# A two-layer network on one Trainium2 core: the MLP down-projection by 7 block products in 18 passes, its right operands split on chip, and the activation differences made on GpSimd

## Chip, core and metric

The kernel runs on 1 core of one Trainium2 chip. The metric is device time in microseconds (us) of one launch; the time before is the median of 3 runs. Engines are named as in the profile: PE is TensorE (matmuls), PEld its weight load, DVE VectorE, ACT ScalarE, POOL GpSimd, and SP the engine that issues most DMAs. A name with q behind it is that engine's queue.

## What is computed

The input is one sequence of 1024 tokens with width 1024, float32. Two residual layers and a mixed-attention block follow one another:

```python
for i in range(2):
    mod = silu(c) @ ada_w[i] + ada_b[i]
    sh1, sc1, g1, sh2, sc2, g2 = split(mod, 6)
    h = modulate(rmsnorm(x, norm_mix_g[i]), sh1, sc1)
    x = x + g1 * mixer_i(h)                # pooling in layer 0, a gated spatial unit (SGU) in layer 1
    h = modulate(rmsnorm(x, norm_mlp_g[i]), sh2, sc2)
    x = x + g2 * (square(relu(h @ mlp_w1[i])) @ mlp_w2[i])
x = rmsnorm(x, final_g)
x = x + attention_block(x)                 # two kinds of attention, 16 heads
out = rmsnorm(x, final_norm_gain)
```

The MLP is 1024 to 4096 to 1024. Every large product is made in three matmuls: both operands are split into a rounded high part (type fp32r) and the rest, and hi*hi, hi*lo and lo*hi are added up in PSUM.

## The kernel before

All activations lie transposed in SBUF: width on the partitions in 8 row tiles of 128, tokens along the free side in two halves of 512. One program per engine is written by a common walk over the steps (`walk`, from the middle of the file), and the order on each engine is the order of the calls in it. Semaphores carry all waits. The stage buffer `stage` has 4 slots of 1 MB and takes weights in the order of the walk.

**Up stage** (`fast`, 14 phases a layer). h @ w1 is made per 256 hidden columns as a 2x2 block product by 7 products instead of 8 (`PRODUCTS`, L47, the Winograd form of Strassen's method). The right sides are quarters of h and four sums T1 to T4 of them, made once a layer. The left sides are four quarters of the weight unit and sums S1 to S4, made on DVE (L1953) in every phase. ACT rounds each left side (L1389), DVE makes its low part (L1932). DVE joins the products in PSUM and SBUF (L1970), ACT applies relu and the square (L1408, L1410) and rounds (L1413), DVE makes the low part (L1976), and SP stores both parts to `hidden` in HBM (L871), 512 KB per tile. The first two units of a layer (`first_up`, `first_tile`) are made in the plain way. A phase is 84 matmuls.

**Down stage** (`down`, 16 chunks a layer). Chunk c takes 256 rows of w2 and the two hidden tiles of each half (`MB`, already in high and low parts) and makes 16 output tiles, each with 6 matmuls (L2341 to L2343), in 4 PSUM banks. DVE adds each to the residual, X = X + gate * product (L2035): 256 a layer. ACT and DVE split the weight unit once a chunk (L1223, L1696). 1536 matmuls a layer. In layer 0 SP also brings the modulation weights of layer 1 in chunks 1 to 14 (`late`): 16 units of 1 MB, each of which DVE takes in two instructions of 1024 columns (L1674, L1677), and `mods` on PE (L2362) sums them over the partitions. In the last chunk the squares, sums and statistics of the next norm are made between the output tiles (`completed`).

**Around it.** `norm` scales each of the 16 tiles on DVE (L1853), ACT rounds it (L1259), DVE makes the low part (L1861). Behind the MLP of layer 0 come the value columns of the SGU (`values`, L2656 to L2658, 384 matmuls: 8 token tiles, two units of weights for each of two column halves, statistics on DVE at L2047), then `spatial`, four rounds of `gates` and `mix`, and `project`. Behind the MLP of layer 1 come the heads of the attention block.

The wait that matters on PE in `fast` is this one: the fifth and sixth of the PE products wait for what DVE has joined.

```python
if q == 4:
    pe.wait_ge(first_copied, g + 1)
if q == 5:
    pe.wait_ge(joined, 5 * g + 2)
if q == 6:
    pe.wait_ge(joined, 5 * g + 3)
```

Of the kernel before, what the change touches and what calls it, by code (L numbers as in the profile page):

```python
# [18 lines left out]
P = 128  # L19
S = 1024  # L20
# [25 lines left out]
SUMS = ("T1", "T3", "T2", "T4")  # L46
PRODUCTS = (("S1", "T1", "D", True), ("A11", "B11", "A", True), ("S2", "T2", "B", True), ("S3", "T3", "C", True),  # L47
            ("A12", "B21", "A", False), ("A22", "T4", "C", False), ("S4", "B22", "D", False))
BLOCKS = (("22", 1, 1), ("11", 0, 0), ("21", 1, 0), ("12", 0, 1))
# [22 lines left out]
for _name, _n in (("ident", P), ("tri", P), ("pairs", P), ("rot", P), ("invc", 4 * 16)):  # L72
# [8 lines left out]
         "combine first_up first_tile fetch ops fast fetched_ada fetched_split finish").split()  # L81


class Tally:
# [3 lines left out]
    def __init__(self):  # L88
        self.n = dict.fromkeys("u w c uc un a d t h b q s st n sp ada mod x g o ol r v v2 vg f".split(), 0)
        self.reg, self.per = None, {}  # L90
        self.lead = 0
        self.stored = [0] * SLOTS
# [24 lines left out]
    def loop(self, eng, count, per, body):  # L117
# [6 lines left out]
        for name in self.n:  # L124
            assert name == "uc" or self.n[name] == start[name] + per.get(name, 0), name
            self.n[name] = start[name] + count * per.get(name, 0)

# [8 lines left out]
def build(nc, x_in, cols_in, const_in, ada_w, pool_w, sgu_in, sgu_ws, sgu_bs, sgu_out, w1, w2,  # L136
# [4 lines left out]
    def sb(name, shape, dt=F32, at=None):  # L141
# [3 lines left out]
        if at is None:  # L145
# [25 lines left out]
    MB = sb("MB", [P, 2, FT, NH, 2 * H], F32R)  # L171
# [16 lines left out]
    m_slot = {"22": sb("slot22", [P, 2, H], F32R, at=x_at + 12 * S), "11": sb("slot11", [P, 2, H], F32R, at=x_at + 20 * S),  # L188
              "21": sb("slot21", [P, 2, H], F32R, at=x_at + 28 * S), "12": sb("slot12", [P, 2, H], F32R, at=acc_at + 4 * S)}
    m_full = {"22": sb("full22", [P, H], at=x_at + 16 * S), "11": sb("full11", [P, H], at=x_at + 24 * S),  # L190
              "21": sb("full21", [P, H], at=acc_at), "12": sb("full12", [P, H], at=acc_at + 2 * S)}
    U1 = sb("U1", [P, H], at=x_at + 18 * S)
    U2 = sb("U2", [P, H], at=x_at + 26 * S)
    first_full = sb("first_full", [P, 2, H], at=acc_at)
    first_slot = sb("first_slot", [P, 2, H], F32R, at=acc_at + 4 * S)
    S_sum = sb("S_sum", [P, H], at=acc_at + 8 * S)
    later_full = sb("later_full", [P, 2, H], at=x_at)
    later_slot = sb("later_slot", [P, 2, H], F32R, at=x_at + 4 * S)
# [23 lines left out]
    w_at = m_at + 32 * S  # L222
    rows = sb("rows", [1, 2, D], at=w_at + 4 * UNIT)
# [45 lines left out]
    hidden = nc.dram_tensor("hidden", (F // P, NH, P, 2 * H), F32).ap()  # L269
# [33 lines left out]
    def down_tile(c, i):  # L303

        first = 3
        if c > 0:
            return i // KT, i % KT
        if i < 2 * first:
            return i // first, i % first
        return (i - 2 * first) // (KT - first), first + (i - 2 * first) % (KT - first)  # L310

# [4 lines left out]
    def first_places(i):  # L316

        full, slot = (first_full, first_slot) if i < 4 else (later_full, later_slot)
        return full[:, i % 2, :], slot
# [14 lines left out]
    def hidden_tiles(c, hf):  # L334

        return MB[:, c % 2, :, hf, :].bitcast(F32), hidden[2 * c:2 * c + 2, hf].rearrange("f p n -> p f n")

# [24 lines left out]
    def ada_total(l, cc):  # L362

        return X[:, 2, :] if (l, cc) in ((0, 5), (1, 0), (1, 1)) else acc[:]

    def stats(hf, order="down"):

        return PS_ALL[:, 5, :] if order == "pooled" and hf == 1 else (B6, A[:, 1, :])[hf]

    def pair_of(hf, v):  # L370

        return stats(hf)[:, 0:8].rearrange("p (t v) -> p v t", v=2)[:, v, :]
# [4 lines left out]

    def sums(order, hf):
        return SUM if order == "down" or hf == 0 else SUM2
# [53 lines left out]
    x_loaded = [sem(f"x_loaded{k}") for k in range(KT)]  # L433
# [36 lines left out]
    qk_loaded = [sem(f"qk_loaded{i}") for i in range(2)]  # L470
    v_loaded = [sem(f"v_loaded{i}") for i in range(2)]
    bias_loaded = [sem(f"bias_loaded{i}") for i in range(2)]
# [2529 lines left out]
```

## Time and profile before

| what | us |
|---|---|
| median of 3 runs (lowest, highest) | 2523.53 (2520.54, 2524.2) |
| span of the profiled execution | 2519.7 |
| PE busy | 2460.9 (98%) |
| DVE busy | 1636.2 (65%) |
| ACT busy | 986.4 (39%) |
| POOL busy | 273.9 (11%) |
| the chain that ended last, on PE | 87% |

The span runs from the first to the last instruction of one execution; for that execution no other time is listed, so the span is set beside the runs. Matmuls overlap one another, so a PE duration of 0.39 us is a latency, and what a matmul costs is the distance from its start to the next one's. The same holds in part for DVE and ACT.

### The profile page before, as it was taken

What the parts mean: (1) busy time and instruction counts of PE and PEld (TensorE: products, weight loads), DVE (VectorE), ACT (ScalarE), POOL (GpSimd) and SP (SyncE); (2) the same over time, 40 slices, a digit from 0 to 9 for tenths busy, and PEclk for the clock granted to TensorE, in tenths of its full rate; (3) what the DMA queues carried; (4) which work ended last, traced back from release to release, by engine and by line L of the source; (5) the groups of instructions that cost most, each with busy time, mean ns of one, the idle gap of its engine ahead of it and who ended that gap; (6) DMA issues with size and microseconds to landing.
All of it is one profiled execution on the core that took longest, in us unless ns stands there. A gap on an engine that the chain in (4) does not pass through costs nothing.

```text
span 2519.7 us, 32563 instructions
## 1 busy us (share of the span) xinstructions
PE 2460.9 (98%) x11616; PEld 2003.8 (80%) x11616; DVE 1636.2 (65%) x2554; ACT 986.4 (39%) x1622; POOL 273.9 (11%) x279
## 2 busy tenths in 40 slices
PE   7999999999999999999999999999999999999998
PEld 2588888788887888888888888888888897886677
DVE  7798776777776343458667666666651226998873
ACT  2366565000003232237666300001431226887851
POOL 0200000000002000100000000000010002557731
PEclk9899999999999999999999999999999999999999
DMA  8726666855543610333544844431334472346621
GB/s 306 267 76 234 226 223 260 317 190 178 200 167 108 178 46 1 134 117 142 192 159 167 317 176 140 145 134 51 126 121 146 143 184 71 85 111 160 168 68 67
DMA packets 219076, 396.89 MB, mean 158 GB/s; under 512 B 59440, under 2 KB 136368, under 8 KB 218928
## 3 DMA queue, kind: packets, MB, share of 16 engines
q1 hardware_dynamic: 203696, 336.21, 40.3%
q10 hardware_dynamic: 15232, 58.72, 6.4%
q8 instruction: 91, 1.49, 0.2%
q14 instruction: 57, 0.47, 0.1%
HBM read 285.83 MB, written 115.08 MB: 159 GB/s over the span
## 4 chain that ended last, share of the span: by engine, by line
PE 87%; DVE 5%; issue 3%; POOL 3%; ACT 1%; DMA 0%; DVEq 0%; POOLq 0%; ACTq 0%; SPq 0%
PE banks L2341 23%; PE banks L2343 23%; PE banks L2342 23%; PE banks L2432 2%; PE banks L2871 2%; PE banks L2889 2%; PE banks L2656 1%; PE banks L2657 1%; PE banks L2658 1%; POOL probs L1139 1%; PE banks L2495 1%; DVE neg_max L2278 1%; PE banks L2373 1%; PE banks L2858 1%; PE banks L2859 1%
## 5 line engine op out<-in xcount | busy, mean ns | idle before, releaser
L2035 DVE SCALAR_TENSOR_TENSOR X<-banks,mod,X 128x512 f32<-128x512 f32 x512 | 380.8, 749 | 227.2 <-PE banks L2343 227.0
L2341 PE MATMUL banks<-Hhi,Whi 128*128 128x512 f32 x1248 | 493.3, 395 | 6.6 <-DVE Hlo L1861 2.9
L2342 PE MATMUL banks<-Hlo,Whi 128*128 128x512 f32 x1248 | 486.8, 390 | 0.0
L2343 PE MATMUL banks<-Hhi,Wlo 128*128 128x512 f32 x1248 | 486.8, 390 | 0.0
L2341 PE MATMUL banks<-MB,Whi 128*128 128x512 f32 x1024 | 401.5, 392 | 2.2 <-DVE X L2035 2.2
L2343 PE MATMUL banks<-MB,Wlo 128*128 128x512 f32 x1024 | 399.5, 390 | 0.0
L2342 PE MATMUL banks<-MB,Whi 128*128 128x512 f32 x1024 | 399.4, 390 | 0.0
L1223 ACT ACTIVATE Whi<-stage 128x2048 fp32r<-128x2048 f32 x59 | 112.9, 1913 | 615.3 <-PE banks L2343 577.2
L2341 PEld LDWEIGHTS banks<-Hhi,Whi 128*128 128x128 f32 x1248 | 235.1, 188 | 59.6 <-issue 8.3
L2342 PEld LDWEIGHTS banks<-Hlo,Whi 128*128 128x128 f32 x1248 | 235.1, 188 | 50.4 <-issue 2.4
L2343 PEld LDWEIGHTS banks<-Hhi,Wlo 128*128 128x128 f32 x1248 | 234.9, 188 | 49.4
L2341 PEld LDWEIGHTS banks<-MB,Whi 128*128 128x128 f32 x1024 | 192.9, 188 | 42.5 <-issue 3.0
L2343 PEld LDWEIGHTS banks<-MB,Wlo 128*128 128x128 f32 x1024 | 192.8, 188 | 40.4
L2342 PEld LDWEIGHTS banks<-MB,Whi 128*128 128x128 f32 x1024 | 192.9, 188 | 39.2
L1696 DVE TENSOR_TENSOR Wlo<-stage,Whi 128x1024 fp32r<-128x1024 f32 (+1 forms) x93 | 145.2, 1562 | 89.6 <-ACT Whi L1223 88.1
L1139 POOL TENSOR_SCALAR probs<-probs,rden 128x1024 f32<-128x1024 f32 (+2 forms) x128 | 118.3, 924 | 337.3 <-DVE rden L2284 327.6
L2289 DVE TENSOR_TENSOR PTl<-banks,PTh 128x512 fp32r<-128x512 f32 (+2 forms) x256 | 135.2, 566 | 6.6 <-ACT PTh L1609 5.5
L2871 PEld LDWEIGHTS banks<-const,probs 128*128 128x128 f32 x800 | 88.6, 140 | 56.8 <-DVE PTl L2289 22.6
L2341 PE MATMUL banks<-T,Whi 128*128 128x512 f32 x336 | 131.1, 390 | 0.0
L2871 PE MATMUL banks<-const,probs 128*128 128x128 f32 x800 | 116.5, 279 | 14.7 <-POOL probs L1139 9.2
L1609 ACT ACTIVATE PTh<-banks 128x512 fp32r<-128x512 f32 (+2 forms) x256 | 119.5, 504 | 29.1 <-PE banks L2871 26.2
L2343 PE MATMUL banks<-T,Wlo 128*128 128x512 f32 x336 | 130.8, 389 | 0.0
(247 smaller groups left out, 3773.2 us busy)
## 6 DMA issues: line engine op xcount, KB each, us to landing
stage<-w SPq DMA_DIRECT2D x64, 1024.0 KB, 6.1
hidden<-slot SPq DMA_DIRECT2D x112, 512.0 KB, 3.0
MB<-hidden ACTq DMA_DIRECT2D x56, 1024.0 KB, 5.6
stage<-ada_w SPq DMA_DIRECT2D x48, 1024.0 KB, 6.5
x_saved<-X SPq DMA_DIRECT2D x32, 512.0 KB, 3.1
stage<-w_in SPq DMA_DIRECT2D x13, 1024.0 KB, 6.2
X<-x_saved SPq DMA_DIRECT2D x24, 512.0 KB, 7.2
MB<-hidden SPq DMA_DIRECT2D x8, 1024.0 KB, 10.1
```

Source lines behind the costliest of these rows:

```text
L1139: nc.gpsimd.tensor_scalar(out=row, in0=row, scalar1=rden[:, u % 4:u % 4 + 1], scalar2=1.0, op0=ALU.mult, op1=ALU.mult).then_inc(probs_scal ...
L1223: nc.scalar.activation(Whi[:, T.n["w"] % 2, :], stage[:, s, :], ACT.Copy).then_inc(w_hi, 1)
L1609: nc.scalar.activation(probs_t(PTh, u, kind, first, m), TP[:, g, 0:m * P] .rearrange("p (k q) -> p k q", q=P), ACT.Copy).then_inc(th_done, 1)
L1696: ins = nc.vector.tensor_tensor(Wlo[:, w % 2, at], stage[:, u % STAGES, at], Whi[:, w % 2, at].bitcast(F32), ALU.subtract)
L2035: nc.vector.scalar_tensor_tensor(out=X[:, k, half(hf)], in0=Dn[:, i % D_BANKS, :], scalar=gate[:, k:k + 1], in1=X[:, k, half(hf)], op0=ALU ...
L2289: nc.vector.tensor_tensor(probs_t(PTl, u, kind, first, m), TP[:, g, 0:m * P].rearrange("p (k q) -> p k q", q=P), probs_t(PTh, u, kind, fir ...
L2341: nc.tensor.matmul(out_bank, whi, xhi, start=start, stop=False, skip_group_check=onto)
L2342: nc.tensor.matmul(out_bank, whi, xlo, start=False, stop=False, skip_group_check=onto)
L2343: return nc.tensor.matmul(out_bank, wlo, xhi, start=False, stop=stop, skip_group_check=onto)
L2432: ins = nc.tensor.matmul(row_bank(cc, h), c_act[:, 2 * q + k:2 * q + k + 1], stage[:, u % STAGES, k * D + h * H:k * D + (h + 1) * H], star ...
L2871: ins = nc.tensor.transpose(TP[:, g, k * P:(k + 1) * P], PE_[:, u % 2, a:a + P], con("ident"))
L2889: ins = nc.tensor.matmul(OB[:, g % 2, :], VT[:, e, k, :], x[:, g % 2, k, :], start=k == tiles[0] and x is PTh, stop=k == tiles[-1] and x i ...
```

## The change

The down-projection becomes a 2x2 block product too. An output block pair `o` (4 of them) is 256 rows of the width by 1024 tokens; a pair `p` (16 of them) is 256 rows of w2. A pass makes the 7 products of one `o` over 2 to 4 `p`, and adds them to X and to a running sum UT. 18 passes of 42, 63 or 84 matmuls make 1344 a layer. The right sides are now stored unsplit, 7 tiles of 256 KB a pair (B11, B21, B22 and T1 to T4), brought back one by one (`load_raw`, a ring of 8) and split on chip: ACT rounds, DVE makes the low part. The four differences T1 to T4 of the up stage's results are made on POOL (on DVE for the first two units), and so are the weight sums S1 to S4 of each pass. Modulation vectors 2, 3 and 4 of layer 1 move to the value stage of the SGU, and vector 5 into the up stage of layer 1. The norm behind the down stage begins after the last pass.

```diff
+PASSES = ((0, 0, 2), (1, 0, 3), (2, 0, 4), (3, 0, 4), (0, 2, 6), (1, 3, 7), (2, 4, 8), (3, 4, 8), (0, 6, 10),
+          (1, 7, 11), (2, 8, 12), (3, 8, 12), (0, 10, 14), (1, 11, 14), (2, 12, 16), (0, 14, 16), (1, 14, 16),
+          (3, 12, 16))
...
+def made_during(p):
+    return -1 if p < 2 else p - 2 if p < 4 else max(t for t in range(NPASS) if PASSES[t][1] <= p - 4 < PASSES[t][2])
+def right_steps(t):
+    pairs = [p for p in range(CHUNKS) if made_during(p) == t]
+    steps = [[] for _ in range(len(SIDES) + 1)]
+    for n, p in enumerate(pairs):
+        for q in range(len(SIDES)):
+            steps[min(q + 2 * n, len(SIDES))].append((p, q))
+    return steps
...
+            for t in range(NPASS):
+                do["passes"](T, gate, l, t, base, then)
...
         do["values"](T, 0, range(1))
+        for q in range(4):
+            ada(1, 2, q)
         split(src_values(1, 0))
         do["values"](T, 0, range(1, 8))
+        for q in range(4):
+            ada(1, 3, q)
         split(src_values(1, 1))
         do["values"](T, 1, range(5))
+        for q in range(4):
+            ada(1, 4, q)
         split(src_in(sgu_in, 0))
...
+            if j < 3:
+                mods(1, 2 + j)
...
+            def load_raw(T, l, n):
...
+                    sync.wait_ge(right_lo, split_by(l, p0, q0))
+                side_stored(l, p, q)
+                sync.dma_start(raw_tile(T, n), hidden[p, q]).then_inc(raw_in[n % RAW], 16)
...
@@ SP @@
+            def passes(T, gate, l, t, base, then):
+                if t + 2 < NPASS:
+                    load_pass(T, l, t + 2)
+                if t == 0:
+                    sync.wait_ge(m_square, 4 * g + 1)
+                    sync.wait_ge(joined, 5 * g + 3)
+                    reload_row(3)
+                    for n in range(4):
+                        store_sum(PAIRS - 1, g, n)
...
+                    for k, b, name in ((4, "22", "T2"), (5, "11", "T1"), (7, "21", "T4")):
+                        sync.wait_ge(b_stored[b], 16 * (g + 1))
+                        sync.wait_ge(t_stored[name], 16 * (g + 1))
+                        reload_row(k)
+                for n in LOADS[t]:
+                    load_raw(T, l, n)
...
@@ POOL @@
+            def fast(T, l, p, base, unit, last):
+                for n in range(4 if p > 0 else 0):
+                    hidden_sum(T.n["f"] - 1, n)
+                if last:
+                    pass_sums(T, l, 0, ("S1", "S3", "S2", "S4"))
@@ POOL @@
+            def passes(T, gate, l, t, base, then):
+                if t + 1 < NPASS:
+                    pass_sums(T, l, t + 1, ("S1", "S3", "S2"))
+                    for n in range(4 if t == 0 else 0):
+                        hidden_sum(g, n)
+                    pass_sums(T, l, t + 1, ("S4",))
...
@@ ACT @@
+            def passes(T, gate, l, t, base, then):
...
+                for q in range(len(SIDES)):
+                    act.wait_ge(pass_done, 7 * (NPASS * l + t) + q + 1)
+                    if q == 1 and t == FIRST_PASS[o]:
+                        nc.scalar.activation(UT[:, o, :], fast_bank("A", t), ACT.Copy).then_inc(u_begun, 1)
+                    if t + 1 < NPASS:
+                        pass_hi(T, l, t + 1, base, q)
+                    for p, r in steps[q]:
+                        right_hi(T, l, p, r)
...
@@ DVE @@
+            def passes(T, gate, l, t, base, then):
...
+                for q, name in enumerate(("D1", "A1", "B", "C1", "A2", "C2", "D2")):
+                    if name in evictions(t):
+                        evict(l, t, gate, name)
+                    if q == 2 and last:
+                        for more in ("U21", "U12", "U22"):
+                            evict(l, t, gate, more)
+                    if t + 1 < NPASS:
+                        pass_lo(T, l, t + 1, base, q)
+                    for p, r in steps[q]:
+                        right_lower(T, l, p, r)
...
@@ PE @@
+            def passes(T, gate, l, t, base, then):
+                if t == 0:
+                    pe.wait_ge(joined, 5 * T.n["f"])
...
+                for q, (_, side, bank, first) in enumerate(PRODUCTS):
+                    pe.wait_ge(ps_lo, 7 * n + q + 1)
...
+                    if q == 4:
+                        if t == FIRST_PASS[o]:
+                            pe.wait_ge(u_begun, OUTS * l + t + 1)
...
+                    if q == 5:
+                        pe.wait_ge(evicted, evicted_by(l, t, "C1"))
```

## Rows read from the trace of the kernel before

**Rows 1.** The page: busy time by engine, and the granted clock in 40 slices.
```profile
PE 2460.9 (98%) x11616; PEld 2003.8 (80%) x11616; DVE 1636.2 (65%) x2554; ACT 986.4 (39%) x1622; POOL 273.9 (11%) x279
PEclk9899999999999999999999999999999999999999
```

**Rows 2.** Stretches: us, busy us by engine (instructions), granted clock, DMA share, GB/s.
```profile
437.86:803.87 366.01, 362.29 (x1625) 300.26 (x1623) 263.13 (x330) 42.08 (x36) 15.57 (x11) 0.99 0.54 192
803.87:810.64 6.77, 3.83 (x25) 3.59 (x25) 6.77 (x12) 4.92 (x9) 1.53 (x2) 0.86 0.97 335
1419.20:1780.16 360.96, 360.96 (x1649) 300.89 (x1648) 228.61 (x298) 43.07 (x38) 0.00 (x0) 1.00 0.42 153
```

**Rows 3.** Groups on PE; then two PE starts, 35 matmuls apart.
```profile
L2341 PE MATMUL banks<-MB,Whi 128*128 128x512 f32 x1024 | 401.5, 392 | 2.2 <-DVE X L2035 2.2
437.86 0.39 PE L2341 MATMUL banks<-MB,Whi 128*128 128x512 f32 x1
445.79 0.39 PE L2343 MATMUL banks<-MB,Wlo 128*128 128x512 f32 x1
```

**Rows 4.** Groups on DVE: instructions, busy us, mean ns, idle before.
```profile
L2035 DVE SCALAR_TENSOR_TENSOR X<-banks,mod,X 128x512 f32<-128x512 f32 x512 | 380.8, 749 | 227.2 <-PE banks L2343 227.0
L1976 DVE TENSOR_TENSOR slot<-full,slot 128x512 fp32r<-128x512 f32 x112 | 77.0, 687 | 41.6 <-ACT slot L1413 41.6
L2289 DVE TENSOR_TENSOR PTl<-banks,PTh 128x256 fp32r<-128x256 f32 x96 | 37.6, 418 | 4.5 <-ACT PTh L1609 3.5
L1677 DVE SCALAR_TENSOR_TENSOR acc<-stage,c_act,acc 128x1024 f32<-128x1024 f32 x24 | 31.7, 1322 | 0.9
```

**Rows 5.** Groups on ACT, and the subtractions' nearest kin on POOL.
```profile
L1389 ACT ACTIVATE Whi<-stage 128x512 fp32r<-128x512 f32 x112 | 69.6, 621 | 41.0 <-PE banks L2343 40.8
L1077 POOL TENSOR_TENSOR SUM<-SUM,SQ x38: 1266/1288/2252, 91.1 to 2503.6; 128x512 f32<-128x512 f32 x38
L1132 POOL TENSOR_TENSOR ws<-ws,const 128x128 f32<-128x128 f32 x8 | 3.4, 461 | 37.2 <-DMA bs<-sgu_bs 37.2
```

**Rows 6.** Timeline: DVE instructions that start beside one on POOL.
```profile
1844.66 1.28 DVE L2227 TENSOR_TENSOR RF<-COS,RT 128x512 f32<-128x512 f32 x1
1844.10 1.29 POOL L1125 TENSOR_TENSOR COS<-QN,rope 128x512 f32<-128x512 f32 x1 [6.84 <-DVE QN L2217]
783.42 2.17 DVE L1696 TENSOR_TENSOR Wlo<-stage,Whi 128x1024 fp32r<-128x1024 f32 x1
780.89 8.69 POOL L1077 TENSOR_TENSOR SUM<-SUM,SQ 128x512 f32<-128x512 f32 x5 [0.80 <-ACT SQ L1239]
```

**Rows 7.** DVE timeline in one up phase with a modulation unit.
```profile
361.93 1.28 DVE L1674 SCALAR_TENSOR_TENSOR X<-stage,c_act,X 128x1024 f32<-128x1024 f32 x1
371.00 0.69 DVE L1970 TENSOR_TENSOR U<-banks,U 128x512 f32<-128x512 f32 x1 [0.40 <-PE banks L2343]
380.96 1.28 DVE L1674 SCALAR_TENSOR_TENSOR X<-stage,c_act,X 128x1024 f32<-128x1024 f32 x1
```

**Rows 8.** DMA issues: number, KB each, us from issue to landing.
```profile
q_heads<-OL SPq DMA_DIRECT2D x16, 256.0 KB, 2.3
X<-x_saved SPq DMA_DIRECT2D x16, 256.0 KB, 3.5
stage<-ada_w SPq DMA_DIRECT2D x48, 1024.0 KB, 6.5
```

**Rows 9.** DVE timeline in the value stage: statistics and weight splits.
```profile
855.85 0.69 DVE L2047 BATCH_NORM_STATS2 bstat<-V 128x6 f32<-128x512 f32 x1 [2.03 <-ACT V L1452]
857.66 2.29 DVE L1696 TENSOR_TENSOR Wlo<-stage,Whi 128x2048 fp32r<-128x2048 f32 x1 [1.11 <-ACT Whi L1223]
891.21 0.69 DVE L2047 BATCH_NORM_STATS2 bstat<-V 128x6 f32<-128x512 f32 x1 [12.91 <-ACT V L1452]
```

**Rows 10.** PE timeline: end of the values, start of the gates; a restart after idling.
```profile
898.55 1.88 PE L2620 MATMUL banks<-ws,ones 128*128 128x512 f32 x4
899.87 0.80 PE L2341 MATMUL banks<-Hhi,Whi 128*128 128x512 f32 x1
116.12 0.77 PE L2341 MATMUL banks<-Hhi,Whi 128*128 128x512 f32 x1 [2.91 <-DVE Hlo L1861]
119.24 0.42 PE L2342 MATMUL banks<-Hlo,Whi 128*128 128x512 f32 x1
```

More of the change, by code:

```diff
@@ L597, in walk, with mlp @@
         T.n["un"] = T.n["u"]
-        def mlp(l, with_ada, after, then):
+        def mlp(l, after, then):
             base = T.n["c"] % 2
@@ L1075, in add_squares @@
                     reach(pool, stat_done, T("st", 2 * hf if order == "down" else 0))
-                first = SQ[:, (i - 1) % 2, :] if k == 1 else acc_sum[:]
-                nc.gpsimd.tensor_tensor(acc_sum[:], first, SQ[:, i % 2, :], ALU.add).then_inc(sum_done, 1)
+                if order == "blocks" and hf == 1 and k == 1:
+                    pool.wait_ge(evicted, evicted_by(T.n["e"] // NPASS, LAST_PASS[OUT_ORDER[1]], "U22"))
+                before = sq_tile(order, i - 1) if k == 1 else acc_sum
+                nc.gpsimd.tensor_tensor(acc_sum, before, sq_tile(order, i), ALU.add).then_inc(sum_done, 1)
             def constant_term():
@@ new lines, in passes @@
+            def passes(T, gate, l, t, base, then):
+                g = PAIRS * (l + 1) - 1
+                if t + 1 < NPASS:
[3 more added lines that the diff above has]
+                    pass_sums(T, l, t + 1, ("S4",))
+                if then == 2:
+                    for n, o in enumerate(OUT_ORDER):
+                        if t == min(LAST_PASS[o] + 1, NPASS - 1):
+                            for i in range(4 * n, 4 * n + 4):
+                                add_squares(T, "blocks", i)
@@ L1204, in attend_end @@
                 gated(T, -1, KT - 1)
-            walk(pool, dict(start=start, pool=pool_step, down=down,
+            walk(pool, dict(start=start, pool=pool_step, fast=fast, passes=passes,
                             spatial=spatial, project=project, heads=heads, attend=attend,
@@ L1349, in project, with block_square @@
+            def block_square(T, l, i, then):
+                act.wait_ge(evicted, finished(l, i))
+                square(T, "blocks", i, then == 4)
             def project(T, j, gate, first, then=None):
@@ L1638, in attend_end @@
                 lower_half(T, -1)
-            walk(act, dict(start=start, prepare=prepare, v_a=v_a, split=split, fetched_split=split, opening=opening,
-                           norm=norm, pool=pool, down=down, values=values, gates=gates,
+            walk(act, dict(start=start, prepare=prepare, v_a=v_a, split=split, opening=opening,
+                           norm=norm, pool=pool, passes=passes, values=values, gates=gates,
                            combine=combine, first_tile=first_tile, ops=ops, fast=fast,
@@ L1882, in norm @@
                                             ALU.subtract).then_inc(gap_ready, 1)
-                    invert(T, 0)
-                for n in range(begun, 2 * KT + 2):
-                    if n == (6 if order == "pooled" else begun + 2):
+                invert(T, 0, which == 4)
+                for n in range(2 * KT + 2):
+                    if n == (6 if order == "pooled" else 2):
                         invert(T, 1, which == 4)
@@ L2469, in norm @@
                 if which == 4:
-                    both_stats(T, 14)
-                    both_stats(T, 15)
+                    for i in range(12, 2 * KT):
+                        both_stats(T, i)
                 elif order == "pooled":
                     pooled_seven(T, 1)
-                    pe.wait_ge(tb_ready, T("b"))
-                    spread(T, 0, B7)
+                elif order == "blocks":
+                    for hf in range(NH):
+                        first_seven(T, order, hf)
+                        eighth(T, order, hf)
                 else:
```

664 lines of the change are left out of this document (410 added, 254 removed).

## The prediction

> **What bounds the kernel.** I read the busy times first: PE is busy for 98% of the span at a granted clock near full speed, the next engine, DVE, for 65% [rows 1]. The stretches then say that this holds in the stage that changes: in layer 1 the down stage lasts 360.96 us with PE busy throughout, and DVE is busy for 228.61 of them [rows 2]. So matmuls taken out there are time, as long as DVE, ACT, POOL and the loads keep up. PE's list shows what one costs: 35 starts in 7.93 us, 0.227 us each, not the 0.39 us of its duration [rows 3]. The other engines' groups give the prices of the work put in [rows 4, 5].
>
> **What is removed.** 1536 - 1344 = 192 matmuls a layer, 384 x 0.227 = 87.2 us off PE. On DVE 256 additions to X a layer become 134 (seven a pass, less four that ACT makes, and three more where each of the four outputs ends), but each pass adds 7 low parts of weights, and eleven passes add 7 (three of them 14) low parts of right sides.
>
> **The up stage.** DVE loses four low parts a phase, ACT four roundings; POOL gains four differences. A POOL instruction of 512 columns is 1.29 us [rows 5]. DVE and POOL do not run freely side by side: a DVE subtraction of two SBUF tiles that began 0.56 us after a POOL product took 1.28 us where its kind takes 0.69, and ended 0.55 us after POOL did; one of 1024 columns took 2.17 us beside five POOL additions, which themselves took 8.69 us [rows 4, 6]. So the four differences, early in the next phase, can hold DVE for up to 4 x 1.15 = 4.6 us. Phases follow at 380.96 - 361.93 = 19.03 us [rows 7]. The join of the fourth product started at 371.00, 0.40 us after DVE was free, and the product that waits for it was due some 2.4 us later; two low parts ahead of it (1.2 us) are gone. 0.4 + 1.2 + 1.8 = 3.4 us of slack against 4.6: a slip of up to 1.2 us in each of the 16 phases that have a modulation unit (12 in layer 0, 4 now in layer 1); the other phases have 2.6 us more slack and slip by nothing. I take 0.5 us, as part of the 4.6 falls where DVE waits anyway: **+8** (0 to 20).
>
> The Trainium skill (SBUF — State Buffer, Who interferes with whom) states that the pair of ports is locked for a whole instruction, and that the later of a two-input DVE instruction and a GpSimd reader fully blocks. By that rule the slip is the full 1.2 us, +19 in place of +8; the pair at 1844 agrees with it, to 0.13 us.
>
> **The start of the down stage.** In the last phase POOL makes its four differences (from about 2.9 us into the phase, 4 x 1.33) before S1 of the first pass, so ACT's first rounding comes at 9 us where it was free at 3, and all operands behind it are late: about 3 us at the sixth product. PE also waits for the last join (0.2 + 0.69 us). **+4** a layer (1 to 8).
>
> **Pass 0.** Here I expect the largest loss. SP's program of this pass puts the four stores of the last differences, and waits for three of them to have landed, ahead of the first raw tile of pair 2. ACT has that tile in its order at step 0, ahead of the copy that starts UT, and PE's fifth product waits for the copy. From the start of the pass: S2 of the next pass is made at 3.9 us (product 1.4, rounding 0.6, low part 0.6, POOL 1.1), four differences to 9.2, the last store landed at 11.7 (2.3 for 256 KB [rows 8]), three row loads and the raw load issued by 12.4, landed at 15.9 (3.5 [rows 8]), ACT's two instructions to 17.1. The fifth product was due at 5.4: 11.7 us of idling, and some 2.5 more at the sixth, since DVE then has four right sides and three left sides to make up. **+14** a layer; 0 if these waits are met early, 20 if the raw tile queues behind three 512 KB rows.
>
> **Passes 1 to 17.** A pass of n pairs is 21n matmuls: 9.5, 14.3 or 19.1 us. DVE's instructions in a row cost 0.66 us (addition), 0.61 (512 columns) or 0.35 (256; durations 749, 687, 418 ns [rows 4], less 0.07 of overlap). Pass with n = 4 and 7 right sides: 4.6 + 4.3 + 4.3 = 13.2, or 18.5 with all of POOL's four sums (5.3) against it: covered. With 14 right sides (passes 3, 7, 11): 17.4 to 22.7 against 19.1. Pass 1: 12.6 to 17.9 against 14.3; pass 13 13.2 to 18.5 against 14.3. Pass 16 is short and ends an output: 10.9 to 16.2 against 9.5. Summed, the least is 1.4 and the most 25 us a layer; I take **+8** in layer 0, where POOL's norm additions lie in the last passes, and **+6** in layer 1. ACT stays under DVE throughout (0.62 us each [rows 5]).
>
> **Ends of the down stages.** Before, layer 0 ran 437.86 to 803.87 and then 6.77 us to the next matmuls [rows 2], 372.8 together, with four modulation sums of PE (7.4) and statistics in it. After: 305.1 (1344 x 0.227) + 4 + 14 + 8 + 7 for the last addition, square, statistics, root, spread and first tile, + 1.3 for DVE's scaling of the second half = 339.4; the sums move, 7.4, and three of them now wait 0.8 us for ACT's evictions: 349.2. **-23.6**. Layer 1: 360.96 + 2.6 of statistics = 363.6; after 305.1 + 4 + 14 + 6 + 9.7 (12 statistics) + 6.6 = 345.4: **-18.2**, of which 4 us are given back because the norm begins only after the last pass.
>
> **Value stage.** DVE gets 12 units of 2 x 1.26 us there. PE asks for the fourth weight unit at 866.6, 48 x 0.227 = 10.9 us after its half begins at 855.7; before, its low part was done at 857.66 + 2.29 [rows 9]. Now four units (10.1) stand ahead of it, and its load starts only when the first of them frees its slot (856.5 + 2.5), lands 6.5 us later [rows 8], and ACT 1.9 and DVE 2.3 follow: 869.9 where 866.6 was due, **+3.3**. The gates' unit has to follow the statistics of 891.21 [rows 9] and four units: 891.9 + 10.1 + 2.3 = 904.3, where the gates began at 899.87 [rows 10]: **+4.5**. Together +8 (0 to 14); nothing on PE covered it.
>
> **Clock.** After 2.91 us of idling PE's matmuls came 0.43 us apart for eight of them, twice the normal distance: the 1.2 GHz level in place of 2.4 [rows 10]. Such a restart costs 1.6 us; I count three: **+5**.
>
> **Sum.** 2519.7 - 23.6 - 18.2 + 8 + 8 + 5 = 2498.9 of span; the median of the runs stands 3.8 above the profiled span: **2503 us**, 0.8% less.
>
> **Rivals.**
> - The forecast: a fifth of the 87 us stays, the rest goes into fixed places, pass 0 first. Chance 0.47.
> - The first pass does not stall, because the differences are early or the stores land fast, and PE restarts less: 2503 - 28 - 5 = 2470. For it: stores of this size land in 2.3 us at a DMA share of 0.42 [rows 2, 8]. Against it: POOL's order and SP's put everything in one line. Chance 0.21.
> - A wash: everything given back, pass 0 at 18 us and the other passes at 12 a layer: 2503 + 8 + 10 = 2521. For it: the queues behind 512 KB rows. Against it: two terms have to be high together. Chance 0.13, of which 0.11 within 0.2%.
> - Slower by the port: each POOL difference holds DVE where it has no slack. The point is the join of the fourth product: if it starts later than 13 us into a phase, PE slips one for one. One POOL instruction of 1.29 us lost in each of 26 phases (33.5, 8 counted) and 0.65 in 26 passes (17): 2503 + 42 = 2545. For it: 2.17 us in place of 1.22. Against it: unaided phases have 6 us of slack. Chance 0.19. The row at 783.42 shows 0.95 us of such holding [rows 6]. By the lock rule of the Trainium skill (SBUF — State Buffer, Who interferes with whom) every POOL instruction that reads SBUF holds such a DVE instruction in full, which leads to this case.
>
> Faster means by over 0.2% (5 us, about what a measurement of this kernel can tell). Faster 0.68, same 0.11, slower 0.21. The range 2470 to 2540 leaves out the far ends of the second and last case.
>
> **What would show it.** After: 2688 matmuls in the passes, and PE waiting for UT's copy (ACT) in the first pass, over 10 us a layer; ACT waiting there for a DMA from hidden; the join rows of 1.2 us and more in the up stage; PE waiting for DVE's weight split twice in the value stage; gaps of some 5 us in passes 1, 15 and 16. The forecast is wrong if the first pass of a layer lasts under 12 us, or if PE idles by over 1 us a phase in the up stage.

## The result, and the profile after

The changed kernel takes 2567.57 us (median, 2562.71 to 2570.25), the kernel before, run beside it, 2522.86 us. The ratio is 1.0175 with a 95% interval of 1.016 to 1.0189: slower by 1.75%, where 2503 us, faster, was predicted, with 2540 as the upper end. The profiled execution has a span of 2564.1 us, 44.4 more than before.

The page of the changed kernel, its busy times and the granted clock, answers to [rows 1]:

```profile
PE 2419.3 (94%) x11232; PEld 1958.2 (76%) x11232; DVE 1708.7 (67%) x2610; ACT 1111.1 (43%) x1946; POOL 661.2 (26%) x535
PEclk9899999899998988999999989999999999999999
```

384 matmuls are gone, as the change says. But PE is busy for 94% of a longer span, and the clock row shows eights where it had nines. At 0.227 us each they are worth 87.2 us; so the change costs 131.6 us elsewhere. The stretches of the changed kernel say where (us, busy us by engine, granted clock, DMA share, GB/s). In order: up stage of layer 0, its down stage up to the value columns, the values, gates to project, up and down stage of layer 1:

```profile
116.47:453.79 337.32, 325.28 (x1440) 265.95 (x1440) 278.13 (x337) 167.22 (x287) 90.70 (x56) 0.99 0.50 171
453.79:802.59 348.80, 317.76 (x1393) 260.75 (x1393) 250.76 (x365) 139.59 (x250) 121.41 (x84) 0.96 0.46 153
802.59:912.08 109.49, 94.86 (x391) 76.40 (x390) 66.97 (x80) 31.74 (x38) 5.36 (x8) 0.92 0.64 202
912.08:1144.93 232.85, 227.32 (x1058) 193.16 (x1057) 85.12 (x117) 54.68 (x78) 15.49 (x12) 0.91 0.25 81
1144.93:1468.36 323.43, 314.99 (x1386) 258.87 (x1385) 243.74 (x318) 170.09 (x286) 86.56 (x56) 1.00 0.46 161
1468.36:1824.33 355.97, 328.85 (x1481) 272.26 (x1481) 249.59 (x371) 139.97 (x252) 103.23 (x72) 0.96 0.46 153
```

The same stretches before, with the change that the terms of the prediction gave each and the change that came:

| stretch | before | predicted | measured |
|---|---|---|---|
| up stage, layer 0 | 321.7 | +10 | +15.6 |
| down stage and transition, layer 0 | 372.8 | -37.4 | -24.0 |
| values | 89.2 | +8 | +20.3 |
| gates to project | 206.8 | +7.9 | +26.0 |
| up stage, layer 1 | 312.5 | +7.9 | +10.9 |
| down stage and transition, layer 1 | 363.6 | -22.2 | -7.6 |
| clock, not placed | | +5 | in the above |
| the rest, with the opening | 853.0 | 0 | +3.2 |
| sum | 2519.7 | -20.8 | +44.4 |

Every stretch is worse than its term, and the largest miss, 18 us, is in a stage whose matrices the change doesn't touch. PE's waits (what it waited for: us in total, times, longest):

```profile
PE banks L2651 <- ACT UT L1602: 37.4, 2, 18.9
PE banks L2651 <- DVE U L2241: 17.4, 18, 3.1
PE banks L2651 <- DVE X L2325: 11.2, 8, 3.7
PE banks L2941 <- POOL ws L1379: 8.8, 1, 8.8
PE banks L2977 <- DVE Wlo L1972: 5.9, 1, 5.9
PE banks L2674 <- ACT X L1739: 2.3, 3, 0.8
```

They name four suspects: the copy to UT in pass 0 (foreseen), the joins of the up stage (foreseen, smaller), the spatial weights (not foreseen), and three short waits of 0.8 us in the gates, which look like nothing.

### The profile page after: what moved, and what is told of

It is laid out like the page before. It is cut to its first block, busy times and chain, and to the rows that moved or that the text cites. A ratio compares the mean times of both kernels' runs of the same rounds, so it can differ in the third digit from the quotient of the medians.

```text
span 2564.1 us, 32727 instructions
## 1 busy us (share of the span) xinstructions
PE 2419.3 (94%) x11232; PEld 1958.2 (76%) x11232; DVE 1708.7 (67%) x2610; ACT 1111.1 (43%) x1946; POOL 661.2 (26%) x535
## 4 chain that ended last, share of the span: by engine, by line
PE 71%; DVE 12%; issue 10%; POOL 4%; ACT 2%; DMA 1%; POOLq 0%; DVEq 0%; SPq 0%; ACTq 0%
PE banks L2651 19%; PE banks L2653 19%; PE banks L2652 19%; DVE Wlo L2203 2%; PE banks L3192 2%; PE banks L3210 2%; PE banks L2729 2%; POOL probs L1386 1%; DVE S_sum L2224 1%; PE banks L2793 1%; PE banks L3179 1%; PE banks L3180 1%; DVE U L2241 1%; DVE stage L2224 1%; PE banks L2685 1%
## 5 line engine op out<-in xcount | busy, mean ns | idle before, releaser
L2651 PE MATMUL banks<-Hhi,Whi 128*128 128x512 f32 x1760 | 703.1, 400 | 76.4 <-ACT UT L1602 37.4
L2652 PE MATMUL banks<-Hlo,Whi 128*128 128x512 f32 x1760 | 692.5, 393 | 0.0
L2653 PE MATMUL banks<-Hhi,Wlo 128*128 128x512 f32 x1760 | 692.0, 393 | 0.0
L2652 PEld LDWEIGHTS banks<-Hlo,Whi 128*128 128x128 f32 x1760 | 335.4, 191 | 70.4 <-issue 2.7
L1332 POOL TENSOR_TENSOR slot<-slot,slot 128x512 f32<-128x512 f32 x112 | 180.0, 1607 | 486.3 <-ACT slot L1688 436.7
L2651 PE MATMUL banks<-T,Whi 128*128 128x512 f32 x720 | 282.4, 392 | 3.0 <-DVE full L2241 3.0
L2652 PE MATMUL banks<-T,Whi 128*128 128x512 f32 x720 | 281.0, 390 | 0.0
L2653 PE MATMUL banks<-T,Wlo 128*128 128x512 f32 x720 | 280.9, 390 | 0.0
L2325 DVE SCALAR_TENSOR_TENSOR X<-banks,mod,X 128x512 f32<-128x512 f32 x180 | 134.4, 747 | 93.9 <-PE banks L2653 93.5
L2651 PEld LDWEIGHTS banks<-T,Whi 128*128 128x128 f32 x720 | 135.6, 188 | 31.6 <-DVE full L2241 3.9
L2653 PEld LDWEIGHTS banks<-T,Wlo 128*128 128x128 f32 x720 | 135.7, 188 | 28.7
L2652 PEld LDWEIGHTS banks<-T,Whi 128*128 128x128 f32 x720 | 135.7, 188 | 27.8
```

Source lines behind the costliest of these rows:

```text
L1332: nc.gpsimd.tensor_tensor(out, a, b, ALU.subtract).then_inc(t_sums, 1)
L2325: nc.vector.scalar_tensor_tensor(out=x, in0=source, scalar=gate[:, k:k + 1], in1=x, op0=ALU.mult, op1=ALU.add).then_inc(evicted, 1)
L2651: nc.tensor.matmul(out_bank, whi, xhi, start=start, stop=False, skip_group_check=onto)
L2652: nc.tensor.matmul(out_bank, whi, xlo, start=False, stop=False, skip_group_check=onto)
L2653: return nc.tensor.matmul(out_bank, wlo, xhi, start=False, stop=stop, skip_group_check=onto)
```

## The experiments

All edits are to the changed kernel, so its time, 2567.6, is what they are held against; ratios are to the kernel before. The runs are called e1 to e12. The first four take one suspect each. The interval of a ratio is some 4 us to either side, so a difference of less than some 5 us between two runs is not clear of noise by the times alone; what is said of it rests on the rows.

**Pass 0: a queue, or an engine? (e1)** The chain is read from the timelines of three engines in pass 0 (start, duration, engine, line): the first tile of pair 2 is loaded behind everything else, and ACT, with the copy to UT behind that tile, waits for it.

```profile
461.66 0.99 POOL L1322 TENSOR_TENSOR S_sum<-S_sum,stage 128x384 f32<-128x384 f32 x1 [4.30 <-DVE Wlo L2248]
466.90 1.26 POOL L1332 TENSOR_TENSOR slot<-slot,slot 128x512 f32<-128x512 f32 x1 [0.17 <-POOL slot L1332]
463.90 4.62 SPq L1013 DMA_DIRECT2D hidden<-slot  x4
468.61 2.05 SPq L1017 DMA_DIRECT2D X<-x_saved  x4
470.75 8.15 SPq L1041 DMA_DIRECT2D stage<-hidden  x9
477.20 0.63 ACT L1590 ACTIVATE T<-stage 128x512 fp32r<-128x512 f32 x1 [17.06 <-DMA stage<-hidden]
477.74 0.58 ACT L1602 ACTIVATE UT<-banks 128x512 f32<-128x512 f32 x1
478.46 0.77 PE L2651 MATMUL banks<-Hhi,Whi 128*128 128x512 f32 x1 [18.94 <-ACT UT L1602]
```

```diff
                 if t == 0:
+                    for n in LOADS[0][:8]:
+                        load_raw(T, l, n)
                     sync.wait_ge(m_square, 4 * g + 1)
...
-                for n in LOADS[t]:
+                for n in LOADS[t][8 if t == 0 else 0:]:
```

> Theory (a queue, not an engine): the fifth product of pass 0 waits 18.94 us in layer 0 and 18.45 us in layer 1 for the copy to UT on ACT, because ACT stands before the split of the first raw tile of pair 2, and that tile's load is queued on SP behind the stores of the four late differences and the reloads of X. With the eight loads of raw tiles 14 to 21 put ahead of that block on SP, both waits fall under 2 us, the two of 1.1 and 1.6 us behind them go too, and the clock of pass 0 stays up. Down stage with transition of layer 0 falls from 348.8 to 322 to 328 us, of layer 1 from 356.0 to 329 to 335, the whole by 40 to 48 us against the changed kernel: 2520 to 2528 us, 0.999 to 1.002 of the kernel before. Rival (the four differences and S2, S4 of pass 1 on POOL are the bound): the wait only moves to the first, third or seventh product of pass 1, which then waits 5 to 15 us, and the whole falls by 10 to 25 us to 2543 to 2558 us.

Measured: 2545.88 us, 1.0097 (1.008 to 1.0114), 21.7 us less. The wait for UT fell to 5.2 us in layer 0 and 10.1 in both, the two down stages by 10.9 and 12.9 us. So the queue on SP was most of that wait, but the theory's size was wrong: half came, and the time lies in the rival's range. The wait did not move to pass 1, as the rival had it: what was left, 5.2 us for UT and 3.4 for X in layer 0, was still in pass 0, which took 22.1 us in place of 31.5. The trace of this run shows one thing that I had not looked at: in the first 25 us of the down stage the DMA engines are full (columns as above). They are full in the same place of the kernel before too (second row), where PE never waited: the change puts more waits on the same full engines.

```profile
454.78:480.00 25.22, 16.62 (x56) 12.71 (x57) 18.92 (x26) 10.94 (x22) 12.39 (x9) 0.73 1.00 361
437.86:462.86 25.00, 25.00 (x112) 20.72 (x111) 17.95 (x24) 3.93 (x5) 0.00 (x0) 1.00 1.00 384
```

**The three short waits in the gates (e2).** In each of rounds 0 to 2 PE makes one vector's sums (16 matmuls of one column) between gates and mix.

```diff
-            if j < 3:
-                mods(1, 2 + j)
+            if j == 0:
+                for cc in (2, 3, 4):
+                    mods(1, cc)
```

> Theory (each visit of the modulation sums between gates and mix costs its own time and then a stretch at half clock): gates to project took 232.9 us against 206.8 before, with the matmuls of mix at 9.70, 8.68 and 9.28 us in the three rounds with a visit and 5.30 in the round without. With all three sums made in round 0, rounds 1 and 2 come back to 21.9 for gates and 5.3 for mix: two visits saved, 3.4 and 4.0 us in mix and some 3 in gates, while the first visit grows longer by its two waits. The stretch falls to 218 to 224 us, the whole to 2553 to 2559. Rival (the half clock there has another cause, as the load of weights or the short matmuls of mix): the later rounds stay at 8.7 to 9.3 in mix, and the whole stays within 3 us of 2567.6.

Measured: 2561.02 us, 1.016 (1.0143 to 1.0177), 6.5 us less, and gates to project 226.0; both lie 2 us above the theory's ranges. The rows bear the mechanism out: from first to last start the 48 matmuls of mix took 5.2 us in each round before, 9.5, 8.5, 9.1 and 5.2 after, and here 10.1, 5.2, 5.2, 5.2. The size is short, since the one long visit itself runs mostly at half clock: its 48 matmuls take 9.9 us with 1.0 of waits, where three times 16 took 5.0. The starts in the changed kernel show the fall (PE timeline): 0.11 us apart at first, 0.21 from the eighth on, that is 2.4 and 1.2 GHz.

```profile
936.71 1.92 PE L2674 MATMUL banks<-ones,X 128*128 128x1 f32 x16 [0.78 <-ACT X L1739]
938.63 0.28 PE L2652 MATMUL banks<-WSlo,Vhi 128*128 128x128 f32 x1
938.74 0.27 PE L2653 MATMUL banks<-WShi,Vlo 128*128 128x128 f32 x1
939.45 0.41 PE L2652 MATMUL banks<-WSlo,Vhi 128*128 128x128 f32 x1
939.66 0.41 PE L2653 MATMUL banks<-WShi,Vlo 128*128 128x128 f32 x1
```

**The spatial weights (e3).** SP had issued them at 896.14, behind the weight unit of the gates, which had to wait for a slot of `stage` that the modulation units held; PE asked at 900.5.

```profile
864.72 0.37 SPq L956 DMA_DIRECT2D stage<-ada_w  x1
895.73 0.37 SPq L956 DMA_DIRECT2D stage<-sgu_in  x1
896.14 0.58 SPq L1120 DMA_DIRECT2D ws<-sgu_ws  x1
909.28 3.78 PE L2941 MATMUL banks<-ws,ones 128*128 128x512 f32 x4 [8.76 <-POOL ws L1379]
```

```diff
             ada(1, 2, q)
+        do["spatial_loads"](T)      # SP's two loads, taken out of spatial
         split(src_values(1, 0))
```

> Theory (a queue again): gates waits 8.76 us for the masked spatial weights because SP issues their two loads behind the last of twelve modulation units. With the two loads put behind the first four units on SP, the wait is gone, the two sums over the spatial weights (2.8 us at half clock) fall to about 1.4, and the stretch from the value columns to gates falls from 109.5 to 97 to 101 us: the whole to 2555 to 2559 us. Rival (the transfers only change places): the spatial weights' 1 MB delays the weight units behind them, the wait of 5.9 us for the third weight unit grows by 3 or more, and the whole falls by less than 5 us, to 2563 or above.

Measured: 2557.94 us, 1.0149 (1.0132 to 1.0166), 9.6 us less, as the theory had it, and the value stage 102.5 in place of 109.5, where it had 97 to 101. The queue it was. The stage gained less than forecast, because the gates then wait 3.83 us for their own weight unit.

**Differences on DVE or on POOL (e4).** The timelines of one phase of the changed kernel: three instructions of 0.69 us last 1.78 as long as POOL works, and are 0.69 again when it stops. Joins, which have one input in PSUM, are not held: nine of them ran beside POOL in the block phases of the two layers, and each took 0.68 to 0.69 us.

```profile
353.25 2.20 DVE L1953 SCALAR_TENSOR_TENSOR X<-stage,c_act,X 128x1024 f32<-128x1024 f32 x1
355.37 1.77 DVE L2224 TENSOR_TENSOR S_sum<-stage 128x512 f32<-128x512 f32 x1
357.06 1.78 DVE L2224 TENSOR_TENSOR stage<-stage 128x512 f32<-128x512 f32 x1
358.76 1.78 DVE L2203 TENSOR_TENSOR Wlo<-S_sum,Whi 128x512 fp32r<-128x512 f32 x1
360.64 0.69 DVE L2224 TENSOR_TENSOR S_sum<-S_sum,stage 128x512 f32<-128x512 f32 x1
361.86 0.68 DVE L2241 TENSOR_TENSOR U<-banks,U 128x512 f32<-128x512 f32 x1
352.70 1.66 POOL L1332 TENSOR_TENSOR slot<-slot,slot 128x512 f32<-128x512 f32 x1 [12.90 <-ACT slot L1688]
358.46 1.53 POOL L1332 TENSOR_TENSOR slot<-slot,slot 128x512 f32<-128x512 f32 x1 [0.17 <-POOL slot L1332]
```

```diff
 POOL, fast:
-                for n in range(4 if p > 0 else 0):
-                    hidden_sum(T.n["f"] - 1, n)
 DVE, fast:
                 after(0)
+                if p > 0:
+                    hidden_sum(g - 1, 0)
+                    hidden_sum(g - 1, 1)
                 after(1)
+                if p > 0:
+                    hidden_sum(g - 1, 2)
+                    hidden_sum(g - 1, 3)
```

> The four differences of each block phase but the last are made on DVE again, POOL does nothing in the up stage. Theory (the two engines hold each other up): sums beside POOL took 1272 ns on DVE where they took 685 before. With POOL still they take 680 to 700, the join is in time, and a phase with a modulation unit comes back from 19.97 to 19.0 to 19.3 us: up stage of layer 0 from 337.3 to 324 to 329 us, of layer 1 from 323.4 to 317 to 321, the whole by 10 to 18 us to 2550 to 2558. Rival (DVE's own queue is the bound, not POOL): four more instructions of 0.7 us, 2.8 us a phase, delay the joins, the phases stay at 20 us or grow to 21, and the whole comes out at 2567 to 2585.

Measured: 2553.66 us, 1.0129 (1.0113 to 1.0146), 13.9 us less. DVE does four instructions more a phase and is earlier for it: its sums are back to single price (groups of this run; 1272 ns before this edit), and a phase with a modulation unit lasts 19.04 us, not 19.98. Layer 0's up stage fell from 337.3 to 327.6. In layer 1 the four such phases have their old length again, within 0.22 us, but the first phase became 1.4 us longer and the last 1.0, so its up stage stayed at 323.3 us, where the theory had 317 to 321. Why is open.

```profile
L2232 DVE TENSOR_TENSOR S_sum<-stage 128x512 f32<-128x512 f32 x28 | 19.2, 687 | 1.0
L2232 DVE TENSOR_TENSOR stage<-stage 128x512 f32<-128x512 f32 x28 | 19.1, 684 | 0.0
```

**Do they add up? (e5)**

> The edits of the four runs before it in one kernel: raw loads first, the three modulation sums in round 0, the spatial weights early, the block differences on DVE. Theory (four separate costs): the savings add up, 21.7 + 6.5 + 9.6 + 13.9 = 51.7 us against 2567.6, so 2513 to 2519 us, 0.997 to 0.999 of the kernel before. Rival (they overlap, one cover taken away uncovers another: DVE, with the differences back, meets the raw tiles of the last phase): 2522 to 2535.

Measured: 2516.60 us, 0.9979 (0.997 to 0.9988): 51.0 less, where the single runs sum to 51.7. The match is closer than the intervals allow one to claim, but the rival's 2522 and more lie outside this run's. So these are four costs that hardly overlap, and without them the changed kernel is as fast as the one before or a little faster.

**What is left in pass 0 (e6).** On top of the raw loads put first, the split of pair 2 stands later by two products, and the load of the weights of pass 2 stands behind the eight raw tiles on SP (the second edit is left out here):

```diff
-            steps[min(q + 2 * n, len(SIDES))].append((p, q))
+            steps[min(q + 2 * n + (2 if t == 0 else 0), len(SIDES))].append((p, q))
```

> On top of the raw loads put first: the split of pair 2 stands two products later on ACT and DVE, so that the copy to UT no longer stands behind it, and the 1 MB of weights for pass 2 is loaded behind the eight raw tiles. Theory (queues on ACT and SP are still the bound): the wait for UT, 5.2 us in layer 0, is gone in both layers, and half of the 3.4 for X as well; 2545.9 falls by 10 to 14 us to 2532 to 2536. Rival (the 16 DMA engines are the bound: they were busy all of the first 25.2 us of the down stage at 361 GB/s): the wait only moves to pass 1 or 2, the sum of the waits in the first 30 us of the down stage stays between 6 and 10 us, and the whole between 2541 and 2547.

Measured: 2541.96 us, 1.0084 (1.0068 to 1.0099), 3.9 less than the raw loads alone. The wait for UT fell to 1.8 us in layer 0, but PE waited 7.4 us for additions to X: the sum of the waits stayed (5.2 + 3.6 against 1.8 + 7.4), as the rival had it. Its time is in the rival's range too, and passes 0 and 1 of layer 0 together took 37.1 us, where they took 36.9 with the raw loads alone. That the DMA engines are the reason isn't shown: the edit also reorders ACT and DVE.

**The sums where PE waits anyway (e7).** On top of the early spatial weights:

```diff
+        do["three_mods"](T)    # PE: 24 columns into one bank; DVE: one addition
+        T.add(mod=3)
         do["spatial"](T)
...
-            if j < 3:
-                mods(1, 2 + j)
```

> On top of the spatial weights loaded early: the sums of the three modulation vectors over the partitions are 24 matmuls in one go ahead of the sums over the spatial weights, where TensorE waited 3.83 us for a weight unit anyway, with one addition on DVE. Theory (in gates and mix the cost is what each visit does to the clock behind it): gates to project falls from 232.8 to 207 to 213 us, the value stage grows by 1 to 4, the whole from 2557.9 to 2535 to 2541. Rival (the clock falls there for another reason, as the many short matmuls of mix or the changed start of the stage): gates to project stays above 225, the whole above 2550.

Measured: 2543.74 us, 1.0087 (1.0071 to 1.0102), 14.2 less than with the early weights alone, but 3 above the theory's range. Gates to project is 208.2 at a granted clock of 0.98 (0.91 before the edit), and all four rounds of mix take 5.2 us. So 24.6 of the 26 us in that stretch were the three visits and the clock behind them. The value stage grew by 11.3, not by 1 to 4, which is why the whole missed: at half clock the one visit takes 10.4 us.

```profile
902.34 10.40 PE L2693 MATMUL banks<-ones,X 128*128 128x1 f32 x48 [3.36 <-DVE X L1954]
915.89:1124.10 208.21, 204.62 (x1010) 172.72 (x1009) 83.77 (x114) 55.82 (x79) 15.48 (x12) 0.98 0.24 81
```

**POOL idle in the passes too (e8).** `pass_sums` for passes 1 to 17 moved from POOL to DVE, on top of the differences on DVE.

> On top of the differences on DVE: the sums S1 to S4 of passes 1 to 17 are made on DVE too, so POOL does nothing there but the four late differences. Theory (the shared port costs DVE as much as the sums save it, but the passes have room on DVE): DVE in the passes goes from 75% to 85 to 90% busy, the rest of the passes' waits is unchanged, the whole stays within 4 us of 2553.7. Rival 1 (POOL held the passes up): the waits for UT and X in passes 1 to 17 and the half clock stretch of the last passes of layer 1 go, 2540 to 2548. Rival 2 (DVE becomes the bound): low parts are late in every pass, 2565 to 2590.

Measured: 2550.08 us, 1.0116 (1.01 to 1.0131), 3.6 less than with the differences alone. The waits for UT fell from 38.1 to 28.8 us and those for X rose from 8.5 to 15.6. Two things cancel here. Passes 0 and 1 together became 5.2 us shorter in layer 0 and 3.5 in layer 1, since POOL comes sooner to the late differences; the rest of layer 0's down stage became 6.6 us longer with the sums in DVE's queue, and the rest of layer 1's stayed. POOL did hold DVE in passes 2 to 17: of the low parts of weights of 512 columns, 0.69 us alone, 23 of 80 took over 0.9 in layer 0 of e4, and one of 81 in e8. But in the changed kernel PE waited only once a layer between pass 1 and the last passes, 0.25 us, so the 17 us that a rival of the prediction gave to the port there didn't reach PE.

**Together (e9).**

> The edits of e6 (raw loads first, copy to UT first, weights of pass 2 behind them), e7 (spatial weights early, three sums in one go) and e8 (differences and pass sums on DVE, POOL idle) in one kernel. Theory (costs in different stages add up): 2567.6 - 25.6 - 23.8 - 17.5 = 2500.7, so 2497 to 2505 us, 0.990 to 0.994 of the kernel before. Rival (with the sums on DVE, the low parts of the raw tiles in passes 0 and 1 come later and give the queue's gain back): 2508 to 2520, with waits of PE for X and UT of over 8 us a layer in the first 30 us of the down stage.

Measured: 2512.89 us, 0.9964 (0.995 to 0.9977): 12 us short of the sum, and in the rival's range: these costs do not add up as the first four did. In the first 33 us of the down stage PE waited 7.7 us in layer 0, near the 8 that the rival wanted, and 10.6 us for X at the end of layer 0's passes, where e6 had 5.7.

**The first block phase (e10).** In it DVE makes the four differences of the first unit as well. Edit: `first_sums(T, l, 0, ...)` out of DVE's `fast` into POOL's, with one wait ahead of the fourth join.

> On top of e9: the four differences of the first unit, which DVE made in the first block phase, are made on POOL. Theory (the wait of 3.06 us for U in the first block phase of each layer is DVE's queue): it falls under 0.5 in both layers, with the clock behind it, 5 to 8 us in the whole against the run of e9. Rival (the port and the store of the differences, which the fourth join needs, hold DVE as long): the wait moves to the join behind it, less than 2 us gained, or up to 3 us lost.

Measured: 2508.22 us, 0.9947 (0.9933 to 0.996), 4.7 less than e9. The first block phase went from 23.9 to 21.7 us in layer 0 and from 23.9 to 20.4 in layer 1; the waits for U fell from 7.8 to 4.0. DVE's queue was most of it. The wait of 3.06 us fell to 1.25 in layer 0 (and 0.91 for ACT ahead of it) and 1.04 in layer 1, not under 0.5; in the kernel before it was 1.10 and 0.90.

**DMA, or DVE's order? (e11)** The reloads of rows 4 to 7 of X moved behind raw tiles.

> On top of e9: the reloads of rows 4 to 7 of X, 2 MB, stand behind the raw tiles of pair 3 (rows 4, 5) and in pass 1 (rows 6, 7). Theory (in the first 25 us of the down stage the 16 DMA engines are the bound, 365 GB/s at a share of 1.00): the share in that stretch falls under 0.9, the waits of PE there fall by 2 to 5 us a layer, the whole by 4 to 10 us. Rival (DVE's order is the bound there: low parts, evictions and the splits of the raw tiles in one queue): the share falls but the waits stay, the whole within 2 us of the run of e9, or slower by up to 5 where the rows come too late for passes 2 and 3.

Measured: 2512.63 us, 0.9966 (0.9954 to 0.9978), no different from e9. But this doesn't settle it: the share of the DMA engines in the first 25 us went only from 0.97 to 0.95, not under 0.9, so they were hardly relieved.

**The last version (e12).** The pass sums back on POOL:

> The run of e10 with one part undone: the sums S1 to S4 of passes 1 to 17 are made on POOL again, the block differences stay on DVE and the first unit's differences on POOL. Theory (in the passes DVE's queue is the bound near their end: with the sums on it, PE waited 4.06 and 5.75 us for X in passes 15 to 17 of layer 0, where it waited 1.51 and 3.9 with the sums on POOL): the down stages get back 4 to 10 us together, against some 3 us that POOL's S2 costs in pass 0, the whole 2500 to 2507 us, 0.9915 to 0.994 of the kernel before. Rival (beside POOL, DVE loses as much as it is spared): 2507 to 2512, no different from the run of e10.

Measured: 2502.69 us, 0.9933 (0.992 to 0.9947), 5.5 less than e10, in the theory's range (the intervals of the two overlap). It is faster than both kernels: 0.7% less than before, 64.9 us less than the change as it was made. Its down stages with transition are 337.9 and 340.4 us, gates to project 207.7. What is left of PE's waits in the stages that the change touches, and the first 25 us of the down stage:

```profile
PE banks L2688 <- DVE X L2362: 20.1, 8, 4.7
PE banks L3026 <- DVE Wlo L1996: 6.0, 1, 6.0
PE banks L2688 <- DVE U L2275: 4.2, 4, 1.5
PE banks L2688 <- ACT UT L1619: 2.0, 2, 1.1
442.59:468.00 25.41, 19.83 (x79) 15.75 (x80) 20.81 (x28) 13.00 (x26) 15.61 (x11) 0.93 1.01 366
```

## Why the prediction was wrong

The sign was wrong, not by one mechanism but by the sum of several. The count of what was removed, 384 matmuls, was right. The span was forecast 20.8 us shorter and came 44.4 longer. The 65.2 us between are 28.0 in the two down stages, 18.1 in gates to project, 12.3 in the value stage, 8.6 in the up stages and 3.2 elsewhere, less the 5 of the clock's own term. The step that failed most widely is that term: "Such a restart costs 1.6 us; I count three".

- **Gates to project.** I gave this 7.9 us for work and waits of three visits, and these are 7.7 us (3 x 2.56). The other 18 are matmuls at half rate (e2, e7). A visit of 2.6 us with 16 one-column matmuls was followed by half clock and cost 3.3 to 4.3 us in mix and 1.0 to 2.3 in the next gates, three times, where the prediction counted three restarts of 1.6 us in the whole kernel. Some 1.5 us more are in the first gates, behind the wait for the spatial weights.
- **Clock as a whole.** The mean granted clock fell from 0.992 to 0.969: 2564.1 x 0.031 - 2519.7 x 0.008 = 59 us more of full-speed time withheld, a part of it while PE waited anyway. The term was 5.
- **Up stage.** The mechanism was right: DVE was held for 0.92 + 3 x 1.09 = 4.2 us a phase (4.6 was the bound), and phases without a modulation unit kept their 19.04 us. The step that failed is the halving: of "a slip of up to 1.2 us" I took 0.5, "as part of the 4.6 falls where DVE waits anyway". It didn't: less the slack of 3.4 us, 4.2 leaves 0.8, and a phase lengthened by 0.94 us, at its sixth product (q = 5 in the listed waits, which count from 0). The rule of the Trainium skill (SBUF — State Buffer, Who interferes with whom), a lock held for the whole instruction, gave 1.2, and I didn't take it; the rows beside POOL agree with it, with 1.09 us lost per DVE instruction with two SBUF inputs and none in a join with one input in PSUM. The first block phase, 20.4 us before and 23.8 after in layer 0, had no term; e10 shows that the first unit's differences on DVE were most of it. The last, for which "+4" stood, came 1.7 us longer in layer 0 and 3.5 in layer 1.
- **Pass 0.** The chain came as written, POOL, stores, reloads, raw tile, ACT, copy, but the pass lasted 31.5 us in layer 0 and 31.0 in layer 1, where the terms gave 9.5 + 14. Three of its prices were too low. S2 came at 461.66, 7.9 us into the pass and not 3.9 (whose parts sum to 3.7), because ACT waited for two raw tiles before. The load of the raw tile took 6.4 us from 470.75, not 3.5: the loads of [rows 8] that gave this price were issued at 2412 to 2428 us, in the last stage. At the start of layer 0's down stage, in the same trace, the loads of 512 KB rows of X landed only after 3.7 to 7.8 us, at a DMA share of 1.00. And the waits, 18.94 us and 1.1 at the product behind it, left the clock at a mean of 0.70 from 454.78 to 480.
- **Ends and passes.** With pass 0 mended (e12) the down stages are 337.9 and 340.4, against 335.4 and 341.4 forecast with 14 us of pass 0 in each. So 16.5 and 13 us lie above the other terms. Nearly all of it is still in passes 0 and 1: their 105 matmuls take 37.4 us in layer 0 and 36.5 in layer 1, where 23.8 would do at full clock without a wait. PE's waits of 0.9, 4.7 and 3.0 us are 8.6 of these 13.6 us in layer 0; for the rest the clock is down. At the ends the terms were near. In the changed kernel PE waited 1.5, 2.2 and 3.7 us in the last passes of layer 0, with a granted clock of 0.50 from 765 to 775 us, and hardly at all there in layer 1.
- **Value stage.** The wait for the fourth unit was 5.9 us for 3.3. Of the gates' start the step failed that asked only for their weight unit: SP's next two loads, `ws` and `bs`, stood behind the same modulation units, and PE waited 8.76 us for them. Of the 20.3 us these waits are 14.6; the matmuls behind them at half rate are most of the rest, 4.0 in the values and 1.4 in the sums over the spatial weights.
- **The rivals.** The one on the slower side named the port, at 2545 us, and the range ended below it, at 2540. The port was real in the up stage (13.9 us by e4) and was covered in the passes (e8); even without the differences on POOL the kernel would be slower than before, 2553.7 us. So the result has this rival's sign, but mostly by other causes. Of the two signs that were to show the forecast wrong neither came, as pass 0 was far over 12 us and PE mostly idled by 0.7 us a phase: they could not see a pass 0 that costs too much, nor a stage that the change hardly touches.

What stays open: the 8.6 us of waits in passes 0 and 1 of layer 0 in the last version. DMA at a share of 1.01 and DVE busy for 20.8 of 25.4 us both fit, and e6 and e11 don't part them; a full share alone didn't stop PE in the kernel before. Also open are 3 us in the stages behind the second MLP, and the last block phase of layer 1, 22.4 to 24.4 us in every version, 19.04 before.

## What to carry to other kernels

Before a step is moved, write down what is queued behind it on the issuing queue in the new place and when that is next needed: two of the four costs here were loads that nobody meant to delay. Read a DMA price from rows at the place where the load will stand, at the share that it will meet. And price a hole in PE's work by the matmuls behind it at half rate too, not by the hole alone; between gates and mix a few one-column matmuls were such a hole. Moving them to where PE waited already gained 14.2 us, though the visit itself then took 10.4 us at half clock. Giving work to an idle engine can cost a busy one more than doing it itself: four differences of 0.69 us on DVE (2.8 us) were cheaper than the 4.2 us by which POOL held it up.

## What the hardware showed that I had not expected

- The same visit of 16 one-column matmuls doesn't drop the clock everywhere. In the up stage a phase with one is 1.70 us longer (20.74 for 19.04, in the kernel before and in e4), about what the visit itself takes, and the matmuls behind it are 0.23 us apart; between gates and mix, 8.5 to 9.5 us of mix at half rate followed. What differs in the rows is what follows: matmuls of 512 columns there, of 128 columns here. Whether this is the reason was not tried.
- At half clock the one-column matmuls take 0.217 us each (48 in 10.40) where they took 0.111 (16 in 1.78).
- DVE and POOL hold each other up in both directions: the differences took 1.26 us on POOL in pass 0, while DVE was idle, and mostly 1.53 to 2.06 us in the up stage beside DVE.
